# Scale products of the second block: 9 and 15 weight loads summed in one PSUM bank, with their steps placed in the even and odd layers

## What is computed

```python
sc, scc = jax.nn.silu(c), jax.nn.silu(c_ctx)
sh1, sc1, g1, sh2, sc2, g2 = jnp.split((sc @ ada_w[i] + ada_b[i])[:, None, :], 6, axis=-1)
csh1, csc1, cg1, csh2, csc2, cg2 = jnp.split((scc @ ada_w[i] + ada_b[i])[None, None, :], 6, axis=-1)
hx = modulate(x, norm1_g[i], sh1, sc1)
hc = modulate(ctx, norm1_g[i], csh1, csc1)
```

## Time and profile before

| | us |
|---|---|
| median of 3 runs | 2412.43 (2412.03 to 2413.97) |
| the profiled execution | 2412.22 |
| its span in the trace | 2410.5 |
| PE busy, share of span | 1926.5, 80% |
| DVE busy | 966.3, 40% |
| ACT busy | 710.7, 29% |
| DMA share of one queue (q1) | 61.2% |

### The profile page before, as it was taken

One profiled execution on the slowest core, in us unless ns is written; L12 is line 12 of the kernel. 1 busy time (PEld: TensorE's weight loads), 2 busy tenths in 40 slices (PEclk: granted clock), 3 DMA queues, 4 the chain that ended last, 5 costly groups with the idle time before them and its releaser, 6 DMA issues.

```text
span 2410.5 us, 30262 instructions
## 1 busy us (share of the span) xinstructions
PE 1926.5 (80%) x13238; PEld 1377.4 (57%) x13238; DVE 966.3 (40%) x1730; ACT 710.7 (29%) x1152; POOL 4.1 (0%) x11
## 2 busy tenths in 40 slices
PE   7689998879798999769868888978867765665656
PEld 6589997769678999447644332333255532232323
DVE  6866655666656665354462010101064510100101
ACT  5355444453434444334432000000034410000000
POOL 0000000000000000000000000000000000000000
PEclk9899999799999999989989999999988888888788
DMA  6234454321276445841134999999932379999997
GB/s 246 96 140 162 140 193 181 118 96 71 74 265 229 171 169 199 345 177 74 36 140 188 428 428 427 428 427 428 428 126 105 140 302 428 427 428 427 427 427 325
DMA packets 44787, 606.53 MB, mean 252 GB/s; under 512 B 5104, under 2 KB 5232, under 8 KB 6768
## 3 DMA queue, kind: packets, MB, share of 16 engines
q1 hardware_dynamic: 43488, 597.61, 61.2%
q0 software_dynamic: 880, 4.98, 0.6%
q10 hardware_dynamic: 288, 2.02, 0.2%
HBM read 603.54 MB, written 1.05 MB: 251 GB/s over the span
## 4 chain that ended last, share of the span: by engine, by line
PE 50%; DMA 27%; DVE 14%; ACT 6%; issue 2%; SPq 0%; DVEq 0%; ACTq 0%
PE ps L85 48%; DMA m_last_slot<-moe_down 15%; DMA m_more<-moe_up 9%; DVE m_WL L94 2%; PE ps L88 2%; ACT m_WH L91 1%; ACT m_mix_sc L91 1%; DVE m_od_low L100 1%; DMA m_ring<-ada 1%; DVE m_misc L103 1%; DVE m_wk L94 1%; DVE m_ev L94 1%; ACT m_od_low L91 1%; DVE m_misc L112 1%; ACT L91 1%
## 5 line engine op out<-in xcount | busy, mean ns | idle before, releaser
L85 PE MATMUL ps<-m_ring,m_moe_sc 128*32 128x256 f32 (+1 forms) x2304 | 416.0, 544 | 85.1 <-DMA m_ring<-moe_gate 79.2
L94 DVE TENSOR_TENSOR m_WL<-m_ring,m_WH 128x1024 fp32r<-128x1024 f32 (+1 forms) x277 | 330.4, 1202 | 271.5 <-ACT m_WH L91 270.8
L91 ACT ACTIVATE m_WH<-m_ring 128x1024 fp32r<-128x1024 f32 (+1 forms) x277 | 282.9, 1034 | 124.3 <-PE ps L85 120.9
L85 PEld LDWEIGHTS ps<-m_ring,m_moe_sc 128*32 128x32 f32 (+1 forms) x2304 | 151.7, 143 | 236.2 <-issue 122.2
L85 PE MATMUL ps<-m_more,m_moe_sc 128*32 128x256 f32 (+1 forms) x768 | 208.5, 557 | 82.2 <-DMA m_more<-moe_up 82.2
L85 PE MATMUL ps<-m_nH,m_WH 128*128 128x256 f32 x936 | 238.0, 290 | 15.2 <-ACT m_WH L91 15.2
L85 PE MATMUL ps<-m_nL,m_WH 128*128 128x256 f32 x936 | 237.5, 290 | 9.0 <-DVE m_nL L100 8.8
L94 DVE TENSOR_TENSOR m_nT<-ps,m_nT 128x512 f32<-128x512 f32 (+1 forms) x32 | 17.9, 558 | 558.0 <-PE ps L85 558.0
L91 ACT ACTIVATE m_nT<-ps 128x512 f32<-128x512 f32 (+1 forms) x64 | 31.4, 490 | 622.4 <-PE ps L88 323.9
L85 PE MATMUL ps<-m_last_slot,m_nT 128*32 128x256 f32 (+1 forms) x768 | 184.7, 493 | 30.9 <-DMA m_last_slot<-moe_down 30.9
L85 PE MATMUL ps<-m_more,m_nT 128*32 128x256 f32 (+1 forms) x768 | 187.6, 494 | 18.6 <-ACT m_nT L91 18.6
(11 more groups left out here) (304 smaller groups left out, 3109.7 us busy)
## 6 DMA issues: line engine op xcount, KB each, us to landing
m_ring<-moe_gate SPq DMA_DIRECT2D x64, 2048.0 KB, 19.0
m_ring<-moe_up SPq DMA_DIRECT2D x32, 2048.0 KB, 17.3
m_more<-moe_up SPq DMA_DIRECT2D x32, 2048.0 KB, 21.8
m_more<-moe_down SPq DMA_DIRECT2D x32, 2048.0 KB, 18.0
m_last_slot<-moe_down SPq DMA_DIRECT2D x32, 2048.0 KB, 22.6
m_ring<-ada SPq DMA_DIRECT2D x24, 2048.0 KB, 8.5
m_ring<-ffn_down SPq DMA_DIRECT2D x16, 1408.0 KB, 6.0
m_ring<-ffn_gate SPq DMA_DIRECT2D x10, 2048.0 KB, 8.1
```

The source lines that it names most:

```text
L85: return Issued() if self.dry else self.e.matmul(out, lhsT, rhs, start=start, stop=stop, skip_group_check=skip)
L91: return Issued() if self.dry else self.e.activation(*a, **k)
L94: return Issued() if self.dry else self.e.tensor_tensor(*a)
```

## The change

The 24 steps add up in PSUM bank 7, in two groups: steps 0 to 8 and steps 9 to 23. `c` now stands in two columns of a buffer of zeros (`cz`, 64 columns for each block), and step i takes the 32 columns that put `c` into columns 2i and 2i + 1 of the group, so that each step adds its two rows and zeros elsewhere. The ACT copy, the four transposes and the DVE sums of each step are gone; one copy, four transposes and a few sums for each group stand in the two feed-forward layers. `bg` has three banks until the second block. `spare(n)` takes n steps of the idle generator at a place even if jobs wait: nine in the even layer, one at the start of `mix(0)`, three ahead of `mix(1)`. The silu of `c` moves from the first PLE to the even layer.

```diff
@@
+EARLY = 9
@@ class Jobs
+    def spare(self, n):
+        for _ in range(n):
+            next(self.idle, None)
@@ program
         fg = Ring(banks, [0, 1, 2, 3], at)
-        bg = Ring(banks, [4, 5, 6, 7], at)
+        bg = Ring(banks, [4, 5, 6], at)
@@
-        c2 = c_pad.rearrange("p (k n) -> p k n", k=8)
+        cz = adaT[:, :].rearrange("p (k n) -> p k n", k=8)
+        ada_rows = sb("ada_rows", 512, offset=area + 4 * 17920)
+        ada_groups = [(0, EARLY), (EARLY, 24)]
@@ pe_ada
-            for i in range(25):
-                if i < 24:
+            for group, (a, b) in enumerate(ada_groups):
+                for i in range(a, b):
                     c = W.chunk("ada", (i // 12,), 4 * (i % 12), 4, 8, "raw")
...
-                            ins = pe.matmul(ps[32 * g:32 * g + 32, :].rearrange("p (j n) -> p j n", j=4), c2[:, 2 * g + k, :], w[:, :, 2 * g + k, :],
-                                            k == 0, k == 1)
+                            ins = pe.matmul(banks[7][32 * g:32 * g + 32, :].rearrange("p (j n) -> p j n", j=4), cz[:, 2 * g + k, o:o + 32], w[:, :, 2 * g + k, :],
+                                            i == a and k == 0, i == b - 1 and k == 1, True)
                     ins.then_inc(*P.mark(("ada", i), ("free", c)))
-                if i > 0:
-                    pe_transposes(("adaT", i - 1), [adaT[:, j * 128:(j + 1) * 128] for j in range(4)], [("ada copy", i - 1)], bg, ("ada sum", i - 1))
-                yield
+                    yield
@@ act_ada (and dve_ada in the same manner)
-                    act_copy(adaT[:, :], bank["ada", i][:, :], [("ada", i)], ("ada copy", i))
-                    ada_act[0] += 1
+            for i in range(24):
+                ada_act[0] += 1
                 yield
@@ new, called from pe_ffn(l) at j0 == 12 (act_ada_sums from act_ffn(l) at j0 == 4)
+        def pe_ada_sums(group):
+            pe_transposes(("adaT", group), [ada_rows[:, j * 128:(j + 1) * 128] for j in range(4)], [("ada copy", group)], fg, ("ada sum", group))
+        def act_ada_sums(group):
+            act_copy(ada_rows[:, :], banks[7][:, :], [("ada", ada_groups[group][1] - 1)], ("ada copy", group))
+        def dve_ada_sums(group):
...
+                for s in range(2):
+                    dve.tensor_reduce(m[:, s, :, :], parts[:, s, c0 - a:c1 - a, :, :], AX.X, ALU.add).then_inc(*V.mark(("ada sum", group)))
@@ pe_even (the same calls stand in act_even and dve_even)
             pe_jobs.fill(1)
+            pe_jobs.spare(2)
             for t in range(2):
                 pe_transposes(("qT", t), block4(eq, t), ["q turned"], fg, ("qT out", t))
             pe_jobs.fill(2)
+            pe_jobs.spare(1)
             for t in range(2):
                 pe_transposes(("kT", t), block4(ek, t), ["k turned"], fg, ("kT out", t))
...
             def values(i):
+                pe_jobs.spare((2, 1, 1, 2)[i])
@@ act_even
             run(tokens("qi", eqi))
+            act.wait_ge(*at("c2 zero")).wait_ge(*at("rest landed"))
+            act.activation(cz[:, :, 30:32], sm("c2").rearrange("p (k s) -> p k s", k=8), ACT.Silu).then_inc(*A.mark("c2"))
@@ pe_odd (and act_odd, dve_odd)
             def mix(H):
+                if H == 0:
+                    pe_jobs.spare(1)
...
             pe_jobs.finish()
+            pe_jobs.spare(3)
             pe_jobs.add(out_half(0, bg))
             mix(1)
             pe_jobs.finish()
+            run(pe_jobs.idle)
             run(out_half(1, fg))
@@ pe_program
             pe_ple(1)
-            run(pe_jobs.idle)
+            bg.places, bg.read[7] = [4, 5, 6, 7], ("ada copy", 1)
```

More of the change, by code:

```diff
@@ L677, in pe_ada @@
         def pe_ada():
-            for i in range(25):
-                if i < 24:
+            for group, (a, b) in enumerate(ada_groups):
+                for i in range(a, b):
                     c = W.chunk("ada", (i // 12,), 4 * (i % 12), 4, 8, "raw")
                     w = slots[W.chunks[c][6]].rearrange("p (j k n) -> p j k n", j=4, k=8)
-                    ps, before = bg.take(("ada", i), ("ada copy", i))
-                    pe.wait_ge(*before).wait_ge(*at("c2")).wait_ge(*at(("landed", c)))
+                    pe.wait_ge(*at("c2")).wait_ge(*at(("landed", c)))
+                    if group:
+                        pe.wait_ge(*at(("ada copy", 0)))
+                    o = 30 - 2 * (i - a)
@@ new lines, in dve_ada @@
+            for i in range(24):
+                ada_dve[0] += 1
+                yield
+        def pe_ada_sums(group):
[3 more added lines that the diff above has]
+        def dve_ada_sums(group):
+            a, b = ada_groups[group]
+            dve.wait_ge(*at(("adaT", group))).wait_ge(*at("rest landed"))
+            parts = bank["adaT", group][:, :].rearrange("p (j g i s) -> p s i j g", j=4, g=4, s=2)
+            for l in range(2):
+                c0, c1 = max(a, 12 * l), min(b, 12 * l + 12)
+                if c0 >= c1:
+                    continue
+                m = mods[l].rearrange("p (c j s) -> p s c j", c=12, j=4)[:, :, c0 - 12 * l:c1 - 12 * l, :]
+                for s in range(2):
+                    dve.tensor_reduce(m[:, s, :, :], parts[:, s, c0 - a:c1 - a, :, :], AX.X, ALU.add).then_inc(*V.mark(("ada sum", group)))
+                flat = mods[l][:, 8 * (c0 - 12 * l):8 * (c1 - 12 * l)].rearrange("p (n s) -> p n s", s=2)
+                n0, n1 = 48 * l + 4 * (c0 - 12 * l), 48 * l + 4 * (c1 - 12 * l)
+                dve.wait_ge(*V.now())
+                dve.tensor_tensor(flat, flat, bc(sm("ada_b", n0, n1).unsqueeze(2), [128, n1 - n0, 2]), ALU.add).then_inc(*V.mark())
@@ L898, in act_even @@
             act_jobs.fill(1)
+            act_jobs.spare(2)
             for t in range(2):
@@ L902, in act_even @@
             act_jobs.fill(2)
+            act_jobs.spare(1)
             for t in range(2):
@@ L916, in values @@
             def values(i):
+                act_jobs.spare((2, 1, 1, 2)[i])
                 for j in range(2):
@@ L1060, in dve_even @@
             dve_jobs.fill(2)
+            dve_jobs.spare(1)
             pick(4)
@@ L1536, in act_odd @@
             act_jobs.finish()
+            act_jobs.spare(3)
             act_jobs.add(act_dense(8, 4))
@@ L1539, in act_odd @@
             act_jobs.finish()
+            run(act_jobs.idle)
             run(act_dense(8, 4, squares_of("odd")))
@@ L1690, in dve_odd @@
             dve_jobs.finish()
+            run(dve_jobs.idle)
             run(dve_dense(8, 4, add_x(("od_out", 1), "odd")))
@@ L2421, in act_program @@
             act_ple(1)
-            run(act_jobs.idle)
             for l in range(2):
@@ L2433, in dve_program @@
             dve_ple(1)
-            run(dve_jobs.idle)
             for l in range(2):
```

31 lines of the change are left out of this document (13 added, 18 removed).

## The result

The changed kernel takes 2387.56 us (median of 4 runs, 2382.83 to 2391.89), the kernel before in the same round 2412.23 (2411.62 to 2413.97): a ratio of 0.990, with a 95% interval of 0.9876 to 0.9923. Run once more on another occasion it took 2384.85 (2379.88 to 2394.30) against 2412.54, ratio 0.9899 (0.9873 to 0.9925). Forecast was 2388, in a range of 2363 to 2399. The execution that was profiled took 2382.83, with a span of 2381.5, so the two traces differ by 29.4 us where the medians differ by 24.7.

What follows compares the result with a forecast made beforehand. DMA was taken to bound 990 to 1038 us, the last 11 ada loads. Run-out -48.1, even layer +32.4 and smaller terms sum to -24.5, from 2412.2 to 2387.7, forecast 2388, range 2363 to 2399 (own range 2378 to 2396).

Steps and rivals of the forecast that it cites:

- the run-out of 48 us: Behind the second PLE: the DMA-bound wait for the last 11 ada loads goes, -48.1, bounds -51.5 and -40.
- the first stall: Even layer: zc, issued right behind an ada load, lands at 101.6 and DVE waits, +14.1, bounds 9.6 and 17.
- the second and third: Even layer: zh and zb each wait for the slot of the dense chunk before, +7.2 and +5.2.
- The last two steps: Even layer, `values(3)`: two steps where PE has no wait left, 2 x 1.92 = +3.8, bounds 0 and 6.3.
- Second PLE and run-out: Second PLE to the mixer's start: -48.1 for the run-out and -1.5 for the PLE's step, -49.6.
- The bound of -51.5: Run-out: the gain if the two `m_WH` pieces of `w_in` hide before the second PLE's last square.
- the first PLE's -6.1 for -4.1: First PLE: the step no longer waits for ACT's silu and takes 1.92, -4.1, bounds 0 and -6.
- Odd layer: `mix(1)`: eight sets of transposes of 0.42 go, -3.4; at the end `od_out`'s slot is asked for earlier, -2.5.
- The spare at `mix(0)`: Start of `mix(0)`: the step stands ahead of transposes that all wait for, with PE busy before it, +1.9.
- Rivals 1 and 2: Even layer: 1, only the first stall stands, 2375, chance 0.13; 2, loads are hidden there, 2361, chance 0.08.
- Rival 3: Three banks pinch: PE's background products wait for copies, +5 to +15, 2393 to 2403; chance 0.05.
- Rival 4: Even layer: PE at half clock throughout, +40 there, kernel slower at 2428; chance 0.04.

Runs made afterwards that it cites:

- small loads: Changed kernel with the even layer's nine ada loads cut to 256 of 4096 columns, the rest of their products left out; 2385.43 us, ratio 0.9892.
- the long run of the changed kernel: Changed kernel run again without edit; median 2384.85 us (2379.88 to 2394.30), ratio 0.9899 to the kernel before; the profiled execution was the longest.
- the last experiment: Against the best kernel (one step between dense chunks, silu later), one feed-forward step moved to the odd layer, groups of 8 and 16; 2360.06 us, ratio 0.9789.
- Two edits of 8 and 7 us alone: Against the kernel before: adding up in bank 7 alone, 2404.27 us, ratio 0.997; moved steps and silu alone, without adding up, 2405.64 us, ratio 0.9979.

## Why the prediction was right, and where it wasn't

**The mechanism** was the one forecast: the run-out of 48 us goes, and half of it comes back as refills of a ring of three slots. That the sum hit the median to 0.2 (2387.7 for 2387.56) is luck: the four runs are two of 2383 and two of 2392, with the median between them, and by the traces the sum is 4.8 off. But the experiments confirm its largest terms one by one: the first stall (no stall with one step ahead of zc; 4.5 shorter with small loads), its independence from the second and third, and that order makes them, with 4.5 of the first from the load ahead of it.

**The stalls** were forecast within 0.2 us each, because their terms came from rows that show just that: when the slot was freed, a load's time alone and behind another, and DVE's fixed order.

**The last two steps: +3.8 forecast, +5.9 measured.** The step of the prediction that failed is the sentence that `ev_out`'s refill comes "behind the same pattern (9.15 from 144.8), and PE has work for that long". Two steps of 3.64 together are no cover for 9.15; DVE waited 6.52 for `ev_out`'s first piece. The kernel without these two steps has 1.01 there, and the 5.9 are gone. So the price was a fourth refill and not TensorE's time for two steps. (Its upper bound was too low besides: the 3.15 of the earlier trace rows were at a mean granted clock of 0.59, and the step at 131.82 above, at 0.50, took 3.64.)

**Second PLE and run-out** came out at -49.3 for -49.6, but by errors that cancel. I put the two `m_WH` of `w_in` between the last square and the root (-48.1) and took -1.5 for the PLE. In fact they lie ahead of the last square, so the way to the root is shorter than forecast: -50.1 to the activation that the prediction took, -50.7 to DVE's scaling of the sums behind it. The last period of the PLE's chain is the longer for it, 6.73 for 3.80, +2.9. The bound of -51.5 named this case, and its price for the PLE was not seen. The step that is gone from the PLE gave 0.5 for the 1.5 forecast, and 1.1 there is the clock.

**The trace moved 29.3, the sum says 24.5.** 5.6 of the 29.3 us are the clock, at four places where the code is the same before and after: the projection of the feed-forward layers (-1.5 each) and the statistics at the start of both PLEs (-1.5 and -1.1). Without them the trace moved 23.7, 0.8 from the sum, in which the last two steps (+2.1) and the odd layer (-2.3) again cancel. TensorE waits 2.06 us ahead of either projection, in both kernels, and 0.9 and 0.7 at the start of the first PLE. Before (first fence) and after (second), at the projection of the first feed-forward layer and at the start of the first PLE:

```profile
229.00:236.00 7.00, 6.57 (x40) 6.40 (x41) 2.05 (x4) 3.15 (x5) 0.00 (x0) 0.76 0.62 262
...
383.00:392.00 9.00, 6.38 (x31) 4.86 (x29) 6.36 (x11) 4.84 (x8) 0.00 (x0) 0.81 0.15 62
```

```profile
415.00:424.00 9.00, 7.42 (x57) 5.41 (x55) 7.44 (x11) 5.61 (x9) 0.00 (x0) 1.00 0.28 112
```

The first of them answers the line of 263 to 270 above, at 1.00. In the long run of the changed kernel three of the four are slow again (0.76 at 266 to 273, 0.81 at 421 to 430, 0.83 at 982 to 992), and the second projection stays at 1.00. Of the ten traces of all kernels in which TensorE waits 2.06 us ahead of the first projection, eight have it in 8.0 to 8.1 us and two (the changed kernel's and the last experiment's) in 6.6. So these places belong to the execution and not to the change. The profile shows one execution, and here it was a short one.

Of the first PLE's -6.1 for -4.1, the clock has 1.5, and 4.6 are left for the step.

**Odd layer.** In `mix(1)` a period fell from 7.80 to 7.41 us, 0.39 for the 0.42 forecast for a set of transposes. With the end (-2.2 for -2.5) it is -7.3 for -5.9. The sum counted eight sets, and two more are gone ahead of the periods, for about 2.1. At the first of them DVE had waited for the transposes, to add up the step's sums, before it made products that TensorE waits for; before, and then after:

```profile
662.33 0.26 DVE L103 TENSOR_REDUCE m_misc<-ps 128x4 f32<-128x16 f32 x2 [1.17 <-PE ps L88]
662.62 0.17 DVE L94 TENSOR_TENSOR m_misc<-m_misc,m_small 128x8 f32<-128x8 f32 x1
662.70 0.68 DVE L94 TENSOR_TENSOR m_od<-m_od,m_small 128x512 f32<-128x512 f32 x1
```

```profile
687.08 2.16 DVE L101 SCALAR_TENSOR_TENSOR m_od_low<-ps,m_misc,m_od_low 128x128 f32<-128x128 f32 x8 [1.08 <-PE ps L86]
689.16 0.68 DVE L95 TENSOR_TENSOR m_od<-m_od,m_small 128x512 f32<-128x512 f32 x1
```

The spare at `mix(0)` cost 2.15 for 1.9, and the three ahead of `mix(1)` nothing that shows. For the 1.1 by which the program moves less than that up to the loop, no cause is shown.

**The rivals.** Rivals 1 and 2 (later stalls or all of them soaked up) fall by the waits of DVE. Rival 3, three banks that pinch: no wait of background products for a bank is among the shifts. Rival 4, half clock through the even layer: the granted clock there, stalls and all, was 0.86 to 0.89, near the 0.90 of the earlier trace rows:

```profile
46.00:105.00 59.00, 40.70 (x211) 27.76 (x210) 36.26 (x73) 18.78 (x30) 0.00 (x0) 0.86 0.42 161
105.00:150.00 45.00, 35.31 (x256) 27.99 (x255) 29.50 (x83) 17.46 (x42) 0.00 (x0) 0.89 0.51 210
150.00:196.00 46.00, 36.55 (x275) 30.07 (x273) 22.80 (x41) 15.35 (x29) 0.00 (x0) 0.89 0.71 279
```

The Trainium skill's account of bursts that start at half clock ("TensorE: Matmul & The Clock Gate", section "HAM oscillation — how this bites in real kernels") shows in this kernel at single waits: behind the wait of 10.30 for an ada load the changed kernel's third step, at 98.99, took 3.28 for 1.92, at a granted clock of 0.57, and the short waits above cost 1 to 2 us each. It doesn't hold at each of them, since the same wait of 2.06 leaves the clock at 1.00 in one run and at 0.76 in another. On the table loads the trace goes against the drain that the Trainium skill ("ScalarE: Activation LUTs", section "What ACT_TABLE_LOAD costs") gives: the two and the silu cost 2.5 together, where the prediction's estimate with that drain makes it 4.9 (2.1 and 2.8).

## What to carry to other kernels

With a ring of n slots, filled in a fixed order, count what stands between two chunks that an engine walks through in sequence: with n - 1 loads between them the later one takes the slot of the earlier one and can't be prefetched, however idle the DMA engines are; with n it stands in the list behind the load that takes that slot, which here cost most of all (13.9). Filler loads are hidden best one at a time, which counts for more than whether their compute finds idle time: here nine steps cost the attention layer 34 us in groups of two and three (2.5 of them for the silu), and five cost it 4 us one at a time, with the silu in a wait. Two edits of 8 and 7 us alone (the second with one bank for the steps) gave 25 to 28 together, since one takes away copies, transposes and sums that the other would put in the path (8.4 in one place); test them together, too.

## What the runs showed that was not expected

The same kernel varies by 9 to 14 us between executions (2379.88 to 2394.30), and a trace of a long one against a trace of a short one shows no stage that is to blame: some five places, each 1 to 2.3 us, at which TensorE was granted 0.76 to 0.83 in the one and 1.00 in the other for the same code. A saving of 2 us that is plain in the trace (the silu, the step in `mix(0)`) was not to be seen in medians of four runs.
